# Opening, index selection, table doublings, final norms and scan steps rearranged in a whole-model kernel

## The reference, cut to what matters

```python
for i in range(DEPTH):                       # first_block
    hn = rms_norm(x, ln_attn[i])
    x = x + (moba_attention(hn, ...) if i % N_MIXERS == 0 else dsa_attention(hn, ...))
    x = x + sq_relu_mlp(rms_norm(x, ln_mlp[i]), mlp_w_up[i], mlp_w_down[i])
return rms_norm(x, final_norm)               # then rms_norm_2(x, norm_mix_2[0]) opens the second block

# dsa_attention: which keys a query sees
rel = relu(einsum('bqhd,bsd->bqhs', qi, k_idx32))
score = einsum('bqh,bqhs->bqs', wi, rel)     # masked to earlier keys
_, idx = lax.top_k(score, top_k)             # 64 keys a query
```

## Time and profile before

| | us |
|---|---|
| median of 3 runs | 3037.87 |
| lowest and highest | 3035.69, 3044.16 |
| profiled execution | 3029.94 |
| its span | 3028.0 |
| granted TensorE clock, mean | 0.923 |

### The profile page before, as it was taken

The page is one execution under the profiler, slowest core; times in us unless marked ns, Lnnn a source line. Parts: engine busy times, 40 slices in busy tenths (PEclk is TensorE's granted clock), DMA queues, the critical chain, the costliest instruction groups (busy, mean ns, idle before and its releaser), DMA issues. The chain is left out here.

```text
span 3028.0 us, 37624 instructions
## 1 busy us (share of the span) xinstructions
PE 2609.7 (86%) x13565; PEld 2126.7 (70%) x13566; DVE 1924.2 (64%) x2359; ACT 1516.7 (50%) x1872; POOL 87.2 (3%) x110
## 2 busy tenths in 40 slices
PE   3889985888756769899886988999999899999998
PEld 2668773777635457688765766777787787777777
DVE  2555516687466854455555447887454689888987
ACT  2544424433321134344444436776444677777776
POOL 0000002000013200000010000000000000000000
PEclk8999977999868879899978988999999999999999
DMA  9335530454310144255422416997455699999996
GB/s 242 131 118 191 163 98 28 139 167 154 102 38 2 60 136 153 70 181 195 152 85 84 153 50 235 348 343 281 167 182 189 226 359 330 324 360 334 359 329 222
DMA packets 333549, 566.16 MB, mean 187 GB/s; under 512 B 21913, under 2 KB 126681, under 8 KB 333049
## 3 DMA queue, kind: packets, MB, share of 16 engines
q1 hardware_dynamic: 333432, 564.56, 54.7%
HBM read 558.04 MB, written 6.48 MB: 186 GB/s over the span
## 5 line engine op out<-in xcount | busy, mean ns | idle before, releaser
L1154 DVE TENSOR_TENSOR weights_split<-ring,weights_split 128x1024 fp32r<-128x1024 f32 x676 | 819.0, 1223 | 261.8 <-ACT weights_split L1149 224.6
L1229 PE MATMUL ps<-weights_split,expert_split 128*128 128x512 f32 x3864 | 910.4, 393 | 23.2 <-DVE expert_split L1325 17.7
L1149 ACT ACTIVATE weights_split<-ring 128x1024 fp32r<-128x1024 f32 x676 | 714.8, 1061 | 347.8 <-PE ps L1229 337.3
L1229 PEld LDWEIGHTS ps<-weights_split,expert_split 128*128 128x128 f32 x3864 | 719.8, 188 | 189.1 <-DVE weights_split L1154 35.2
L289 DVE TENSOR_TENSOR weights_split<-ring,weights_split 128x2048 fp32r<-128x2048 f32 x182 | 413.1, 2273 | 453.5 <-ACT weights_split L280 453.2
L280 ACT ACTIVATE weights_split<-ring 128x2048 fp32r<-128x2048 f32 x182 | 344.8, 1896 | 458.4 <-PE ps L460 283.4
L459 PE MATMUL ps<-normed_split,weights_split 128*128 128x512 f32 x1248 | 447.6, 400 | 39.8 <-PEq L342 39.8
L460 PE MATMUL ps<-normed_split,weights_split 128*128 128x256 f32 x1248 | 354.1, 284 | 0.0
L459 PEld LDWEIGHTS ps<-normed_split,weights_split 128*128 128x128 f32 x1248 | 240.3, 193 | 95.6 <-issue 41.6
L365 PE MATMUL ps<-weights_split,hidden_split 128*128 128x512 f32 x1032 | 248.2, 397 | 27.4 <-DVE weights_split L289 19.4
L365 PEld LDWEIGHTS ps<-weights_split,hidden_split 128*128 128x128 f32 x1032 | 194.5, 192 | 72.6 <-issue 22.7
(11 more groups left out here) (366 smaller groups left out, 2344.7 us busy)
## 6 DMA issues: line engine op xcount, KB each, us to landing
ring<-moe_w_gate SPq DMA_DIRECT2D x112, 1024.0 KB, 5.1
ring<-moe_w_up SPq DMA_DIRECT2D x112, 1024.0 KB, 5.1
ring<-moe_w_down SPq DMA_DIRECT2D x112, 1024.0 KB, 5.0
ring<-mlp_w_up SPq DMA_DIRECT2D x32, 1024.0 KB, 5.4
ring<-mlp_w_down SPq DMA_DIRECT2D x32, 1024.0 KB, 4.8
ring<-xa_w_kv SPq DMA_DIRECT2D x16, 1024.0 KB, 5.2
ring<-moba_w_qkv SPq DMA_DIRECT2D x12, 1024.0 KB, 10.7
ring<-da_w_qkv SPq DMA_DIRECT2D x12, 1024.0 KB, 5.1
```

The source lines that it names most:

```text
L1149: nc.scalar.activation(split_piece(p, 0), ring_piece(p), ACT.Copy).then_inc(high.sem, 1)
L1154: nc.vector.tensor_tensor(split_piece(p, 1), ring_piece(p), split_piece(p, 0).bitcast(F32), ALU.subtract)\
L1229: last = nc.tensor.matmul(ps[:, banks[half][tt], :], stationary(s, k, tt), split_piece(p, i)[:, kk * NW:(kk + 1) * NW], start=(opens and n ...
```

## The change

- *Opening.* The three opening stages go. The first norm's stage has all of it: SyncE issues x, constants, two ring tiles, the bias and rows, and then the 24 KB bias row (`ext_dram`, once, no longer 128 times). Ring tiles 2 to 5 are issued in the next stage (`held_from`), where a DMA from DRAM to DRAM spreads the row 128 times (`rows_dram`); tiles 6 and 7 are issued behind it, and then SyncE waits for the spread and issues the skewed read.
- *DSA.* Products and selection are one stage. The index queries come first, then four times a unit of q and four index scores, then k and v; the products use banks 0 to 3 instead of all eight. The index query's weights stand ahead of q's in the ring.
- *Second MLP.* `tables_pool` makes the doublings on GpSimd in one chain of linked instructions, up to 512 elements a partition each. VectorE keeps angles, the first turn (`first_turn`) and coefficients, now by place in the tile order.
- *Final norms.* The gain is loaded in the `ln_mlp` norm stage. `final_norms` multiplies x by it, takes both sums of squares and makes the second norm of x in the same stage.
- *Inverse.* Six mask buffers instead of two; `scan_dve` is cut into `scan_rotate`, called after steps 1, 5, 9, 13 and 17, and `scan_back`, called after steps 7, 11, 15 and 19. GpSimd's `scan_pool` comes after the masks of steps 7, 11, 15 and 19, and at the end. The recurrence calls both halves as before.

```diff
                 if kind == "down":
+                    if beside:
+                        beside.tables_dve(e, i)
...
+        stage(core, pe=pe, act=act, dve=dve, pool=beside.tables_pool if beside else None, uses=len(order))
...
+def final_norms(core, gain, gain_landed, gain_col, scratch, sp):
...
+    def act(e):
+        for tt in range(TT):
+            nc.scalar.activation(xs[:, tt, :], x[:, tt, :], ACT.Square, accum_out=first[:, tt:tt + 1]).then_inc(*sums.up())
+        e.wait_ge(*sums.at(2))
+        nc.scalar.activation(r1, first, ACT.Sqrt, scale=1.0 / D, bias=eps).then_inc(*root.up())
+        e.wait_ge(*gained.at(2))
+        nc.scalar.activation(xs[:, 1, :], xg[:, 1, :], ACT.Square, accum_out=second[:, 1:2]).then_inc(*gained_sums.up())
+        e.wait_ge(*variance.at(1))
+        nc.scalar.activation(r2, r2, ACT.Sqrt, scale=1.0 / D, bias=eps).then_inc(*second_root.up())
+        core.hi(e, core.taken + WS_BUFS)
...
+    def dve(e):
+        V, link = nc.vector, core.link
+        e.wait_ge(gain_landed.sem, 16)
+        V.tensor_tensor(xg[:, 1, :], x[:, 1, :], gain, ALU.mult).then_inc(*gained.up())
+        V.tensor_tensor(xg[:, 0, :], x[:, 0, :], gain, ALU.mult).then_inc(*gained.up())
+        e.wait_ge(*gained.at(2))
+        e.wait_ge(*sums.at(1))
+        link(e, "dve", V.tensor_tensor_reduce(out=xs[:, 0, :], in0=xg[:, 0, :], in1=xg[:, 0, :], scale=1.0, scalar=0.0,
+                                              op0=ALU.mult, op1=ALU.add, accum_out=second[:, 0:1]))
+        e.wait_ge(*root.at(1))
+        link(e, "dve", V.reciprocal(r1, r1))
+        link(e, "dve", V.tensor_tensor(r1_sq, r1, r1, ALU.mult))
+        e.wait_ge(*gained_sums.at(1))
+        V.tensor_tensor(r2, second, r1_sq, ALU.mult).then_inc(*variance.up())
+        e.wait_ge(*second_root.at(1))
+        link(e, "dve", V.reciprocal(r2, r2))
+        link(e, "dve", V.tensor_tensor(r12, r1, r2, ALU.mult))
+        for tt in range(TT):
+            V.tensor_scalar(xs[:, tt, :], xg[:, tt, :], r12[:, tt:tt + 1], None, ALU.mult).then_inc(*scaled.up())
+        for tt in range(TT):
+            V.tensor_scalar(x[:, tt, :], xg[:, tt, :], r1[:, tt:tt + 1], None, ALU.mult)
+        core.lo(e, core.taken + WS_BUFS)
...
-    inverse(core, PB, X, XT, a(22784, 512).rearrange("p (b n) -> p b n", b=2),
+    inverse(core, PB, X, XT, a(22784, 6 * 256).rearrange("p (b n) -> p b n", b=6),
...
-            if n % 4 == 3:
-                mixer.scan_dve(e, n // 4)
+            if n % 4 == 1:
+                mixer.scan_rotate(e, n // 4)
+            if n % 4 == 3 and n > 4:
+                mixer.scan_back(e, n // 4 - 1)
...
-            if n >= 2:
-                e.wait_ge(*w1.at(n - 1))
-            nc.gpsimd.tensor_tensor(q(LM[:, n % 2, :]), LT(b), bc(c(f"level{s}"), 1, 4), ALU.mult).then_inc(*masked.up())
-            if n % 4 == 1 and n > 4:
+            if n >= 6:
+                e.wait_ge(*w1.at(n - 5))
+            nc.gpsimd.tensor_tensor(q(LM[:, n % 6, :]), LT(b), bc(c(f"level{s}"), 1, 4), ALU.mult).then_inc(*masked.up())
+            if n % 4 == 3 and n > 4:
...
-        if n == 3:
+        if n == 5:
+            self.first_turn(e)
+        if n == 6:
             self.coefficients(e)
-        if n == 4:
-            link = self.core.link
-            link(e, "dve", self.core.nc.vector.memset(self.COS[:, :, 0:1], 1.0))
-            link(e, "dve", self.core.nc.vector.memset(self.SIN[:, :, 0:1], 0.0))
-            for level in self.LEVELS[0:3]:
-                self.double(e, level, 0, ST)
-        if n in (5, 6, 7):
-            self.double(e, self.LEVELS[n - 2], 0, ST)
-        if n in (8, 9):
-            self.double(e, self.LEVELS[6], (n - 8) * (ST // 2), ST // 2)
-        if 10 <= n < 14:
-            self.double(e, self.LEVELS[7], (n - 10) * (ST // 4), ST // 4)
+    def tables_pool(self, e):
+        g, link = self.core.nc.gpsimd, self.core.link
+        t1, t2 = self.qt
+        link(e, "pool", g.memset(self.COS[:, :, 0:1], 1.0))
+        link(e, "pool", g.memset(self.SIN[:, :, 0:1], 0.0))
+        e.wait_ge(*self.turn_made.at(1))
+        tt = lambda out, x0, x1, op: link(e, "pool", g.tensor_tensor(out, x0, x1, op))
+        q = (self.co, self.si)
+        for level in self.LEVELS:
+            count = min(ST, 512 // level)
+            for first in range(0, ST, count):
+                which = slice(first, first + count)
+                x1, x2 = (t[:, 0:count * level].rearrange("p (s n) -> p s n", n=level) for t in self.tmp)
+                qc, qs = bc(q[0][:, which], 2, level), bc(q[1][:, which], 2, level)
+                COS, SIN = self.COS[:, which, :], self.SIN[:, which, :]
+                tt(x1, COS[:, :, 0:level], qc, ALU.mult)
+                tt(x2, SIN[:, :, 0:level], qs, ALU.mult)
+                tt(COS[:, :, level:2 * level], x1, x2, ALU.subtract)
+                tt(x1, COS[:, :, 0:level], qs, ALU.mult)
+                tt(x2, SIN[:, :, 0:level], qc, ALU.mult)
+                tt(SIN[:, :, level:2 * level], x1, x2, ALU.add)
+            if level < self.LEVELS[-1]:
+                q2 = (self.qc, self.qs) if q[0] is not self.qc else (self.qc2, self.qs2)
+                tt(t1, q[0], q[0], ALU.mult)
+                tt(t2, q[1], q[1], ALU.mult)
+                tt(q2[0], t1, t2, ALU.subtract)
+                tt(t1, q[0], q[1], ALU.mult)
+                tt(q2[1], t1, t1, ALU.add)
+                q = q2
...
     def scan_dve(self, e, s):
...
+        if s < ST:
+            self.scan_rotate(e, s)
+        if s >= 1:
+            self.scan_back(e, s - 1)
...
-    tiles += feature_tiles(l0["dsa_w_uq"], width=512, raw=True) + feature_tiles(l0["dsa_w_qi"], width=512, raw=True)
+    tiles += feature_tiles(l0["dsa_w_qi"], width=512, raw=True) + feature_tiles(l0["dsa_w_uq"], width=512, raw=True)
...
+    class Opening:
+        x_landed, const_landed, rows_landed = sig("x_landed"), sig("constants_landed"), sig("rows_landed")
+        rows_cleared, cols_ready = sig("rows_cleared"), sig("columns_ready")
+        def sp(self, e):
+            e.dma_start(x[:, :, :], w["x"][0].rearrange("(t p) d -> p t d", p=P)).then_inc(*self.x_landed.up(16))
+            e.dma_start(core.const[:, :], consts).then_inc(*self.const_landed.up(16))
+            core.held_from = WS_BUFS
+            core.issue(e, WS_BUFS)
+            e.dma_start(relb[:, :], w["rel_bias"]).then_inc(*self.rows_landed.up(16))
+            e.wait_ge(*self.rows_cleared.at(1))
+            for dst, src in loads[0]:
+                e.dma_start(dst, src).then_inc(*self.rows_landed.up(16))
+            e.wait_ge(*extd.at(1))
+            e.dma_start(ext_dram, ext_sb[0:H, :]).then_inc(*bias_written.up(16))
...
+        def dve(self, e):
+            nc.vector.memset(core.rows[:, :, :], 0.0).then_inc(*self.rows_cleared.up())
+            e.wait_ge(*self.x_landed.at(16))
+        def dve_parameters(self, e):
+            e.wait_ge(*turned.at(1))
+            nc.vector.tensor_tensor(ext_sb[0:H, :], ps[0:H, 6, 0:CAUS], c("future")[0:H, :], ALU.add)\
+                .then_inc(*extd.up())
+            e.wait_ge(*turned.at(2))
+            nc.vector.tensor_copy(core.cols[:, 0, :], ps[:, 7, 0:P]).then_inc(*self.cols_ready.up())
+        def pe(self, e):
+            e.wait_ge(*self.const_landed.at(16))
+            e.wait_ge(self.rows_landed.sem, 16 * (1 + len(loads[0])))
+            nc.tensor.matmul(ps[0:H, 6, 0:CAUS], relb[:, :], c("onehot")[0:NBUCKET, :], start=True, stop=True)\
+                .then_inc(*turned.up())
+            nc.tensor.transpose(ps[:, 7, 0:P], core.rows[:, 0, :], c("ident")).then_inc(*turned.up())
     def read_bias(e):
+        core.held_from = 10 ** 9
+        core.issue(e, RING)
         e.wait_ge(*bias_written.at(0))
-        skew = bass.AP(ext_dram.tensor, ext_dram.offset + P - 1, [[CAUS - 1, P], [P * CAUS, H], [1, T]])
+        e.dma_start(rows_dram, bc(ext_dram, 1, P)).then_inc(*bias_spread.up(16))
+        core.issue(e, RING + 2)
+        e.wait_ge(*bias_spread.at(16))
+        skew = bass.AP(rows_dram.tensor, rows_dram.offset + P - 1, [[CAUS - 1, P], [P * CAUS, H], [1, T]])
...
+    QI_UNITS, Q_UNITS, K_UNITS, V_UNITS = range(0, 2), range(2, 6), range(6, 10), range(10, 14)
...
+        for u in QI_UNITS:
+            query_unit(u, t0, u * NF, u == 1)
+        for g, u in enumerate(Q_UNITS):
+            query_unit(u, t0 + 1 + g // 2, g % 2 * NF, g % 2 == 1)
+            e.wait_ge(*freed.at(2))
+            e.wait_ge(*columns_kept.at(1))
+            for i in range(4 * g, 4 * g + 4):
+                tt, h = i // IDXH, i % IDXH
+                b0 = 64 * (h % 2)
+                if i >= 4:
+                    e.wait_ge(*relu_done.at(i - 3))
+                nc.tensor.matmul(ps[:, 4 + i % 4, 0:spans[tt][1]], qi(h)[:, tt * P:(tt + 1) * P],
+                                 kiT[b0:b0 + 64, 0:spans[tt][1]], start=True, stop=True).then_inc(*index_scores.up())
+        for g, u in enumerate(K_UNITS):
...
-    stage(core, pe=pe, act=act, uses=3)
...
```

(86 more changed lines are left out.)

238 lines of the change are left out of this document (99 added, 139 removed).

## The result

The changed kernel took 2946.26 us (median of 4 runs, 2942.54 to 2958.93) against 3036.78: ratio 0.9705, 95% interval 0.967 to 0.974. Two later sets, on two chips, gave 2959.57 and 2958.16, ratios 0.975 (0.9733 to 0.9766) and 0.9745 (0.9732 to 0.9759). The forecast was 2960, in a range of 2942 to 2988.

What follows compares the result with a forecast made beforehand. The prediction saw five stages in which no engine is full, and an opening waiting for SyncE's queue; savings of 24 + 16.5 + 16 + 7 + 14 = 77.5 us gave 2952.4 from the profile, 2960.4 from the median; predicted 2960, range 2942 to 2988.

Steps and rivals of the forecast that it cites:

- Opening: Start of the kernel to the first product: 54.0 to about 30, 24 us saved, bounds 20 to 27.
- The copy: DRAM to DRAM spread of the 3.1 MB bias rows beside the q/k/v products: 10 us, no stall, hidden up to 11.
- Products and selection: Both in one stage, the selection running beside the products: 49.9 to 33.4, 16.5 us saved, bounds 14 and 18.
- Doublings: Second MLP stage: table doublings moved from VectorE to GpSimd save 16 us, bounds 0 and 23.
- Contention: Second MLP: VectorE operations waiting for GpSimd ones cost 7 us over ten tile pairs, taken off the 23 us bound.
- Rival (a): Second MLP: GpSimd's chain sets the stage's end at 225 us, the stage gains nothing, time 2976; chance 0.18.
- Norms: Two final norms in one stage with the gain loaded earlier: 21.7 to 14.5, 7 us saved, bounds 5.5 and 8.
- Inverse: Split scan halves and six mask buffers end TensorE's four mask waits: 61.2 to 47, 14 us saved, bounds 8 and 19.
- six masks are ahead: Inverse: six mask buffers, with the rotation two steps earlier, make TensorE's four mask waits (15.2 us) go.
- The rest of the kernel (from 1067 on) is not touched: Two thirds of the span, from 1067 us on, left at its time with no gain or loss.
- rival (c): Opening's DRAM copy: all 16 engines read one row at one's pace, 144 us, time 3093; chance 0.03.

Runs made afterwards that it cites:

- selection_last: Changed kernel with the 16 index scores moved behind all 14 units, so the selection has no products beside it: stage 49.6 us, whole 2972.04 us beside 2958.16.

## Why the prediction was right, point by point

- *Opening*, 24 forecast, 24.7 measured. VectorE ended last, as worked out. The rows landed at 19.2 (19). The copy took 12.0 us where I took 10, between bounds of 9 and 32; its slack is 12.6 (11). So the cover was nearly used up: right, with less room than the text suggests.
- *Products and selection*, 16.5 and 16.9. The stage took 33.0 us (33.4), and `selection_last` shows the mechanism by taking it away.
- *Doublings*, 16 and 19.8. The mechanism was right, the first term was too small: the upper bound of 23 left 3 us of the excess for angles and coefficients. They cost nothing that shows: without the doublings the stage takes 185.8 us with them in it. The doublings cost 26.5 on VectorE: 18.5 in TensorE's waits for low halves (19.7 against 1.2), the rest nearly all in its products, which ran slower in that stage (186.57 us busy at 0.96 against 178.66 at 0.99). Contention was put at 7 and is 6.2. The low halves ran from 2.28 to 3.38 us (2.3 to 3.4), GpSimd was busy for 117.5 (80 to 130), and it ended at 680.6, 17 us before the last product.
- *Rival (a)* would have had the chain end 225 us into the stage, after its last product. The Trainium skill's rule behind it (SBUF — State Buffer, Who interferes with whom: the two engines lock each other out for a whole instruction) agrees with this trace: 215 ns operations of GpSimd took 2.1 to 2.3 us beside a low half. What was wrong was my price for the chain: 512 elements take 1.04 us when alone and not 1.26, and 16 elements 0.22, so it is 71 us and not 81 by itself (my estimate, from the operations that met no lock); it took 126, from 555 to 681. The argument against the rival, that 0.185 us of each GpSimd operation hold nothing, is not borne out: operations of 16 elements waited a low half out too. And by its own sum the rival should have cost more: a chain that ends at 225 us makes the stage 13 us longer than the 211.8 of before, a time of about 2990 and not 2976, just outside the range.
- *Norms*, 7 and 8.2; the split, 6.8 for the gain and 1.4 for the joining, is as the text had it (6.4 from the wait).
- *Inverse*, 14 and 14.3, with one reason too many. The order does all of it; "six masks are ahead" does nothing. I also took 61.2 as this stage's time, which a second profile puts at 65.6. The length with the change came out as worked out (46.9, 47), but the close saving rests on that lucky reading.
- *What was missed.* "The rest of the kernel (from 1067 on) is not touched" passes over the recurrence between the inverse and 1067. It runs the same work and took 7.7 us more, by the clock. No term and no rival held that, nor the 8.0 us of the rest. The five terms together came out low (83.9 measured, 77.5 forecast), and the stages that I left at their time took 12.6 back (7.7 + 8.0 - 3.1), which is why the forecast from the profile came out high (71.3). That 2960 lies within 2 us of the two later medians is in part luck: the two errors offset each other. The first set's median lies 14 us below it, inside the range.
- *Readings.* The profiled execution of before, 3029.94, is not inside the scatter of the three timed ones but 5.7 us below the lowest, and its later stages were short as well. The table write is 2232 KB in 7.7 us, 297 GB/s by that division and not over 300. 14 + 2 + 2 is 18 us for the rows and not 19. The part of the chain that was said to hold nothing is 28 us with its gaps, and not 20. None of these moves the forecast by more than 1 us.
- *Open.* The first set of the changed kernel has three runs at 2942.54 to 2949.24 (mean clock 0.933 or 0.934), the other ten and the profiled one lie between 2955 and 2965 (0.925 to 0.930). Between the medians of the first set and the later ones lie 12 to 13 us. A recurrence at 70.5 would account for 8 of them, but none of the three was profiled.

## What to carry to other kernels

Where one engine's list mixes work for two customers, count the places in the list and not the buffers: a mask behind a waiting scan step comes late with two buffers and with six. When an elementwise chain moves to GpSimd beside VectorE, price it as a lock in both directions: each GpSimd operation that meets a long VectorE one waits it out, each VectorE operation with both inputs in SBUF waits for the rest of one GpSimd operation, and shorter GpSimd operations left VectorE's loss as it was (11.8 us against 11.3), moved it to where TensorE waited less, and made the chain longer. And take a second profile of the kernel before where a stage's clock is below full speed: the same stage read 61.2 and 65.6 us here, and beside a saving of 14 us in it the next stage, with the same work, took 7.7 us more.

## What the runs showed of the hardware

A DMA from DRAM to DRAM that reads each of 16 rows 128 times moved 3.1 MB in 12.0 us behind a full queue, 262 GB/s; the fear of rival (c), all engines at the pace of one, is refuted. From 16 partitions of SBUF the same bytes took 29.7 us, 106 GB/s. Beside a low half of 2.29 us a GpSimd operation of 0.23 us took 2.27, and VectorE's operations with an input in PSUM kept their 0.68. And the granted clock of a stage need not repeat: it did in the recurrence of the changed kernel (78.2, 78.3 and 78.2 us, 0.74 each time) and did not in the inverse of the kernel before (61.2 us at 0.87, 65.6 at 0.78).
